# Chunk mask of two attention groups: written by VectorE, or added by a TensorE matmul

## What is computed

```python
CHUNK = 64
QBLOCK = 128
NEG = -1e30

def blk(args):
    qi, i = args
    qchunk = (i * QBLOCK + jnp.arange(QBLOCK)) // CHUNK
    mask = (kchunk[None, :] <= qchunk[:, None])[None]
    return _attend(qi, k, v, mask, scale)

# _attend, cut
s = jnp.einsum("nqhgd,nkhd->nhgqk", q, k).astype(jnp.float32) * scale
s = jnp.where(mask[:, None, None], s, NEG)
p = jax.nn.softmax(s, axis=-1)
```

## Time and profile before

| | us |
|---|---|
| median of 3 runs | 3233.89 |
| lowest, highest | 3228.85, 3236.66 |
| the profiled execution's time | 3230.68 |
| its span in the profile | 3228.9 |
| TensorE busy in the span | 2901.2 (90%) |
| VectorE busy | 1787.8 (55%) |
| ScalarE busy | 1196.9 (37%) |

### The profile page before, as it was taken

The page is one execution under the profiler, slowest core; times in us unless marked ns, Lnnn a source line. Parts: engine busy times, 40 slices in busy tenths (PEclk is TensorE's granted clock), DMA queues, the critical chain, the costliest instruction groups (busy, mean ns, idle before and its releaser), DMA issues. The chain is left out here.

```text
span 3228.9 us, 49051 instructions
## 1 busy us (share of the span) xinstructions
PE 2901.2 (90%) x19080; PEld 2738.2 (85%) x19080; DVE 1787.8 (55%) x2845; ACT 1196.9 (37%) x2477; POOL 140.3 (4%) x254
## 2 busy tenths in 40 slices
PE   4888879889899999999968888788789999999997
PEld 2787778679899999999947868677789999999997
DVE  5366764643655555554654587465436555545554
ACT  5555644642322212122245565456423222212222
POOL 0200012000000000000002000120000000000000
PEclk8996989889999999999979969898999999999999
DMA  4110001031111111111031100110411111111111
GB/s 178 32 57 30 23 26 41 10 123 45 53 46 46 46 47 40 47 51 42 20 125 47 48 23 21 33 35 11 151 34 46 50 43 46 40 53 46 40 46 62
DMA packets 182277, 161.76 MB, mean 50 GB/s; under 512 B 14488, under 2 KB 169880, under 8 KB 181528
## 3 DMA queue, kind: packets, MB, share of 16 engines
q1 hardware_dynamic: 182040, 158.45, 15.6%
HBM read 129.56 MB, written 29.06 MB: 49 GB/s over the span
## 5 line engine op out<-in xcount | busy, mean ns | idle before, releaser
L1798 PE MATMUL ps<-h_hi,w_hi 128*128 128x352 f32 x2496 | 547.8, 328 | 49.1 <-DVE w_lo L1909 23.0
L1798 PE MATMUL ps<-h_hi,w_lo 128*128 128x352 f32 x2496 | 542.0, 324 | 8.2 <-issue 8.2
L1798 PE MATMUL ps<-h_lo,w_hi 128*128 128x352 f32 x2496 | 540.9, 325 | 0.0
L1798 PEld LDWEIGHTS ps<-h_hi,w_hi 128*128 128x128 f32 x2496 | 427.5, 191 | 65.5 <-issue 44.7
L1798 PEld LDWEIGHTS ps<-h_hi,w_lo 128*128 128x128 f32 x2496 | 431.3, 189 | 0.0
L1798 PEld LDWEIGHTS ps<-h_lo,w_hi 128*128 128x128 f32 x2496 | 427.5, 189 | 0.0
L2249 ACT ACTIVATE cv<-up,cols 128x1058 f32<-128x1058 f32 x88 | 112.0, 1273 | 735.0 <-issue 695.0
L785 PE MATMUL ps<-w_hi,h_hi 128*128 128x256 f32 (+1 forms) x1152 | 335.3, 291 | 24.1 <-DVE w_lo L962 18.2
L786 PE MATMUL ps<-w_lo,h_hi 128*128 128x256 f32 (+1 forms) x1152 | 329.5, 286 | 0.0
L787 PE MATMUL ps<-w_hi,h_lo 128*128 128x256 f32 (+1 forms) x1152 | 327.4, 284 | 0.0
L2360 DVE TENSOR_TENSOR x_t<-ps,x_t 128x1056 f32<-128x1056 f32 x176 | 221.0, 1256 | 159.3 <-PE ps L1798 158.6
(11 more groups left out here) (214 smaller groups left out, 4232.6 us busy)
## 6 DMA issues: line engine op xcount, KB each, us to landing
stage<-in_f_win SPq DMA_DIRECT2D x88, 512.0 KB, 3.8
stage<-in_f_wout SPq DMA_DIRECT2D x44, 512.0 KB, 3.7
stage<-in_w_in SPq DMA_DIRECT2D x40, 256.0 KB, 4.2
x_spill<-x_t SPq DMA_DIRECT2D x2, 4224.0 KB, 13.8
x_t<-x_spill SPq DMA_DIRECT2D x2, 4224.0 KB
stage<-in_w_o SPq DMA_DIRECT2D x16, 512.0 KB, 4.5
w_raw<-in_w_in SPq DMA_DIRECT2D x24, 256.0 KB, 4.0
o_in<-o_spill SPq DMA_DIRECT2D x8, 528.0 KB, 6.9
```

The source lines that it names most:

```text
L1798: last = pe.matmul(ps[:, s0 + b, 0:BAND], lh, rh_[:, b * BAND:(b + 1) * BAND], start=(first_k and n == 0), stop=(last_k and n == 2))
```

## The change

For jobs of B and C that have a mask, TensorE issues one more matmul after the last score matmul. It adds the product of an identity (`ident_r`, 128 x 128, the weights) and a constant (`neg_half`, 128 x 64, rows 0 to 63 are -1e30, the others 0) to the last 64 columns of the job's scores, in the same accumulation group. It is this matmul that now signals `s_done`. VectorE no longer writes the corner for these jobs. Groups A and M are as before. There are 64 such jobs in B and 32 in C per layer, so 192 in all. In the setup VectorE makes the two constants from `ident` in place of the unused `head_mean_w`; it waits for GpSimd's two steps first.

```diff
-    head_mean_w = rc.take("head_mean_w", [P, P])
+    ident_r = rc.take("ident_r", [P, P], F32R)
...
+    neg_half = rc.take("neg_half", [P, 64], F32R)
...
-                dve.memset(head_mean_w[:, :], 0.0).then_inc(S.dve_step, 1)
-                dve.wait_ge(S.dve_step, 1)
-                dve.memset(head_mean_w[0:64, 0:64], 1.0 / HD)
-                dve.memset(head_mean_w[64:128, 64:128], 1.0 / HD)
+                dve.wait_ge(S.pool_step, 2)
+                dve.tensor_copy(ident_r[:, :], ident[:, :])
+                dve.tensor_scalar(neg_half[0:64, :], ident[0:64, 0:64], 0.0, NEG, ALU.mult, ALU.add)
+                dve.tensor_scalar(neg_half[64:P, :], ident[64:P, 0:64], 0.0, None, ALU.mult)
...
                             for m, (qb, kb) in enumerate(pairs):
+                                masked = jb["masks"] and c + n == kn
                                 last = pe.matmul(out, q_st[0:nk, qb, q0:q0 + r], jb["k"][0:nk, jb["k_blk"] + kb, k0 + c:k0 + c + n],
-                                                 start=(m == 0), stop=(m == len(pairs) - 1))
+                                                 start=(m == 0), stop=(m == len(pairs) - 1 and not masked))
+                            if masked:
+
+                                last = pe.matmul(out[:, n - 64:n], ident_r[:, :], neg_half[:, :], start=False, stop=True)
...
-                    for rows, ca, cb in jb["masks"]:
+                    for rows, ca, cb in ([] if one_head else jb["masks"]):
                         link(dve.memset(v[rows, :, ca:cb], NEG))
```

## The result

The changed kernel takes 3268.8 us (median of 6 runs, 3243.6 to 3270.8) beside 3234.8 us of the kernel before (6 runs in the same session, 3228.9 to 3240.7): ratio 1.0087, 95% interval 1.0061 to 1.0113. It is 1% slower, outside the forecast range of 3227 to 3246.5. The kernel before is not steady either: of its 90 executions beside the experiments ten took 3252.8 to 3263.4 us, at a mean granted clock of 0.929 to 0.933 where the others have about 0.94.

What follows compares the result with a forecast made beforehand. TensorE was taken to bound attention C, VectorE B at 2.4 GHz, both nearly full in B at 1.2 GHz. Two layers of 3.8 lost in C less 1.8 gained in B give +4.0 on 3233.9: 3237.9 us, range 3227 to 3246.5.

Steps and rivals of the forecast that it cites:

- C's term: Attention C: all of the mask matmul lies on TensorE's path, a loss of 3.8 us per layer, 1.0 to 4.4.
- one slice more of low clock in C: Attention C: extra time at 1.2 GHz that, with 0.4 us less gain in B, suffices to leave the 0.2% band.
- the second dip: Attention B: the second stretch at 1.2 GHz, 10.3 us, read as beginning behind sparse TensorE work and ending behind dense.
- The mask's price: Each mask matmul costs TensorE 0.11 us at 2.4 GHz and 0.21 us at 1.2 GHz, taken from the values' weight loads.
- The cheap rival: Mask matmul costs only 0.03 to 0.05 us because the next weight load is hidden: 3230.5 us, chance 0.08.
- the clock rises sooner in B: Attention B: denser TensorE work shortens the 1.2 GHz stretches, B gains about 6 us per layer: 3229.7 us, chance 0.15.
- exponent cycle: Attention B, 768 to 1024 keys: a cycle through three engines keeps a pair at 4.01 us despite VectorE's relief.
- the 0.44 us of relief: Attention B: VectorE time freed per pair of jobs by dropping the memsets, 0.22 us per job.
- VectorE's new wait for the scores: Attention B, 896-key pairs: VectorE now idles 0.3 to 0.4 us per pair before a reduction.
- The slow one: TensorE binds in B too, so B gains nothing and C pays 4.4 us per layer: 3242.7 us, chance 0.20.
- relief arriving: Attention B: 13 long pairs gain 0.44 us each, B gains 6.5 us per layer: 3228.5 us, chance 0.09.
- the forecast +4.0: Whole kernel, two layers: C loses 3.8 us and B gains 1.8 us per layer, +4.0 us in all; chance 0.48.

Runs made afterwards that it cites:

- C only: Changed kernel, but the mask goes by matmul only in attention C and B has its memsets back: 3242.1 us, ratio 1.0013.
- wide in C: Changed kernel, but each mask matmul in C moves up to 256 columns, the added ones zeros, instead of 64: 3222.4 us, ratio 0.9953.
- mixed: Changed kernel, but C's jobs up to 384 keys use mask matmuls of up to 256 columns and its longer jobs memsets; B keeps 64 columns: 3219.1 us.
- the shifted kernel: Kernel before, no mask matmul, with the first transpose of C's 12 jobs of 768 to 1024 keys issued twice: 3219.2 us, ratio 0.9953.
- clock alone: Changed kernel, but B and C's longer jobs use memsets; only C's jobs up to 384 keys use a wide mask matmul: 3217.1 us, ratio 0.9938.
- the fastest one: Changed kernel, but mask matmuls of up to 256 columns in B and C's jobs up to 384 keys, memsets in C's longer jobs: 3208.7 us, ratio 0.9917.

## Why the prediction was wrong, point by point

- **C's clock.** The step that failed was unwritten in C's term: "about 9 come before the clock rises at 621.3 us and 23 behind it" takes the moment of the rise from before. It moved from 13.6 us after the fall to 61.4 and 64.9 us. Wide masks put it back and C went from 112.8 to 90.3 us, so this cost 22.5 us in layer 1, nine tenths of C's loss. I had weighed the clock as a rival for B, only upwards, and on the slow side allowed for no more than "one slice more of low clock in C". TensorE in C is the bound, so C was the place where a clock that stays low costs most.
- **The rule behind that rival.** The rows first: 59.75 busy us out of 61.40 did not raise the clock, 8.93 out of 10.30 did. The Trainium skill, "TensorE: Matmul & The Clock Gate", section "The HAM clock gate", says that sustained matmul activity brings full speed. I read activity as busy time, and the second dip seemed to bear that out. In C the busier stretch stayed low, so this reading fails here, and the measurement decides; the runs don't give a better one.
- **The mask's price.** 0.07 and 0.11 us, where I took 0.11 and 0.21 from the values' loads. With an unchanged clock C would have lost 2.6 to 3.1 us, not 3.8: the kernel with 128 columns in the first 12 jobs has the low stretch of before in layer 1, 13.7 us, and its C takes 90.5 us against 87.4. Right in kind, a fifth to a half too large in size. The cheap rival (0.03 to 0.05) was too low. The remark that the float32r loads lie on one line with the FP32 ones is circular, because the line (0.08 + 0.11 each) was drawn through those two rows; a single load of `ident_r` in after takes 0.19 us and fits it.
- **B.** Shorter by 5.9 us, not 1.8. The second low stretch went, which was the first half of the rival "the clock rises sooner in B" (priced there at 1.5 us); the first did not shorten. It need not be the change that took the second stretch away, since C only, with memsets in B, lacks it in layer 2. The long pairs gave 0.18 us each instead of 0.08, so about 1.4 us more over 13 of them. My exponent cycle of 8.02 us, 4.01 per pair, charged each mask matmul at 0.11 us in full and laid its links end to end with rows of before; which link was too long the runs don't tell. Of the 0.44 us of relief 0.18 arrives. A part of the 0.44 was the overlap of two reductions that follow each other, and that is missing here: the two of 345.73 take 2.28 us, more than twice the 1.09 of one. With 1.8 + 1.5 + 1.4 = 4.7 us about 1.2 of the 5.9 stay open. VectorE's new wait for the scores was seen as forecast.
- **Which rival came true.** None. The slow one (TensorE binds in B, 3242.7) is refuted by B's 5.9 us; relief arriving and the clock rising sooner came half true each. If C's clock had stayed, the measured sizes would have given 2 x (2.6 - 5.9) = -6.6 to 2 x (3.1 - 5.9) = -5.6 us and not the forecast +4.0.
- **Not thought of at all.** 9.1 us went with the pauses in the feed-forward stage, which no term covered. Without this luck the change would have cost about 43 us. It also means that every kernel above that shifts TensorE's program holds such a gain beside its own: "wide in C" has 4.8 us of these pauses left, "mixed" 6.2, before 13.8. Against the shifted kernel (3219.2 less its 2.9 us of useless transposes, so about 3216.3) "wide in C", "mixed" and "clock alone" win nothing that is shown, and the fastest one wins some 8 us, with 8.2 us of the pauses still in it.

What stays open: why the low stretch was 30.7 and 34.1 us with memsets in C when B ended sooner. Counted from the fall of the clock, C's first scores come 1.6 and 4.5 us later there, and 2.6 to 2.9 us later in the kernel before and in the shifted one, whose stretches are 13.7 us. A link to the moment at which C starts is thus possible but was not tried by itself. The changed kernel's own runs, 3243.6 to 3270.8 us, fit a rise that comes sooner in some executions (the two fastest have a mean granted clock of 0.935 and 0.933, the other four 0.926 to 0.928), and so do the ten long executions of the kernel before; but only one execution of each kernel has a trace.

## What to carry to other kernels

In a stage that TensorE bounds, a few small matmuls with weights of their own can decide how long the clock stays at 1.2 GHz: their price is what they do to the clock, not their 0.1 us, and here the first 12 jobs of the stage mattered most. Widening such matmuls, even with zeros, can be faster than issuing them narrow: of the 59 executions of kernels with at least 128 columns in those jobs none took over 3227.4 us. And before a difference of half a per cent is put down to an edit, look for pauses without a releaser and for packets of instructions in stages that the edit doesn't touch, and shift the program by a few instructions to see whether they move.

## What the runs showed of the hardware that I had not expected

TensorE stayed at 1.2 GHz for 61 us while busy for 97% of it, and two mask matmuls of 64 columns in place of one of 128 made the difference between 58.0 and 13.7 us of low clock (64.9 and 17.1 in layer 2). Twelve redundant transposes per layer removed 13.8 us of pauses from a stage that starts 150 us behind them, and with them the packets of instructions that queue q8 moved in its later part. The first cost more than anything that the change was meant to gain.
